# The tables of a routed expert layer built one pass later, and its last pair of passes split

## The reference, cut to what matters

```
logits = rms_norm(x) @ w_router + b_router          # 32 experts
top_v, top_e = top_k(logits, 4);  gates = softmax(top_v)
for each token and each of its 4 experts e:
    g, u = split(xn @ w_gu[e] + b_gu[e])            # 1024 -> 2 x 1024
    a = (min(g, 7) * sigmoid(1.702 * min(g, 7))) * (clip(u, -7, 7) + 1)
    y += gate * (a @ w_down[e] + b_down[e])
out = x + y
```

## Time and profile before

| | |
|---|---|
| median of 3 runs | 1271.04 us (1270.73 to 1271.8) |
| profiled execution | 1271.28 us, span 1269.4 us |
| PE busy | 1224.0 us, 96% of the span |
| DVE, ACT, GpSimd busy | 375.8, 193.6, 16.0 us |
| bytes moved | 463.21 MB, mean 365 GB/s |
| chain that ended last | PE 67%, DMA 30% |

### The profile page before, as it was taken

How to read it: one execution, slowest core, us unless ns; L and a number is a source line. 1 busy time by engine, 2 the same in 40 slices (tenths; PEclk the granted TensorE clock), 3 DMA queues, 4 the chain that set the end, 5 groups by cost and what they waited for, 6 DMA issues and landing times.

```text
span 1269.4 us, 16626 instructions
## 1 busy us (share of the span) xinstructions
PE 1224.0 (96%) x6429; PEld 557.6 (44%) x6429; DVE 375.8 (30%) x918; ACT 193.6 (15%) x438; POOL 16.0 (1%) x28
## 2 busy tenths in 40 slices
PE   9999999999999999989898989999999999998997
PEld 5556778685533443333242333334434333432332
DVE  2555755324441221212121212222212221221222
ACT  3223234302301100110001001101000101000001
POOL 0000000011000000000000000000000000000000
PEclk9999999999999999999999999999999999999999
DMA  9787652498699999999999999999999999999994
GB/s 323 188 249 229 233 168 65 141 345 312 235 413 400 423 428 429 426 429 426 429 427 429 425 429 427 427 421 420 426 426 428 428 430 427 426 429 428 427 426 199
DMA packets 79891, 463.21 MB, mean 365 GB/s; under 512 B 20162, under 2 KB 35290, under 8 KB 54882
## 3 DMA queue, kind: packets, MB, share of 16 engines
q1 hardware_dynamic: 75234, 461.50, 89.8%
q10 hardware_dynamic: 4608, 1.05, 0.5%
HBM read 459.53 MB, written 5.09 MB: 366 GB/s over the span
## 4 chain that ended last, share of the span: by engine, by line
PE 67%; DMA 30%; DVE 1%; ACT 1%; issue 1%; SPq 0%; DVEq 0%; POOL 0%; ACTq 0%; POOLq 0%
DMA arena<-w_gu 22%; PE banks L1243 22%; PE banks L1324 9%; DMA arena<-w_down 8%; PE banks L2196 6%; PE banks L630 5%; PE banks L1214 3%; PE banks L1175 2%; PE banks L810 2%; PE banks L1508 2%; PE banks L574 2%; PE banks L1274 1%; PE banks L1196 1%; PE banks L2215 1%; PE banks L686 1%; PE banks L699 1%
## 5 line engine op out<-in xcount | busy, mean ns | idle before, releaser
L1243 PE MATMUL banks<-arena 128*64 128x512 f32 x1984 | 442.5, 596 | 24.4 <-DMA arena<-w_gu 24.2
L1243 PEld LDWEIGHTS banks<-arena 128*64 128x64 f32 x1984 | 136.8, 137 | 301.2 <-issue 245.9
L1324 PE MATMUL banks<-arena 128*64 128x512 f32 x1024 | 226.4, 592 | 4.7 <-DMA arena<-w_down 4.7
L1421 DVE TENSOR_SCALAR arena<-banks 128x512 f32<-128x512 f32 x32 | 22.1, 692 | 386.9 <-PE banks L1243 366.5
L1324 PEld LDWEIGHTS banks<-arena 128*64 128x64 f32 x1024 | 72.8, 136 | 140.3 <-issue 125.3
L1379 ACT ACTIVATE arena<-arena 128x512 f32<-128x512 f32 x32 | 20.2, 630 | 533.1 <-DVE arena L1421 533.1
L2196 PE MATMUL banks<-arena 128*128 128x512 f32 (+1 forms) x192 | 78.0, 562 | 0.9 <-ACT arena L2266 0.9
L1462 DVE TENSOR_TENSOR arena<-banks,arena 128x528 f32<-128x528 f32 x60 | 42.5, 708 | 75.9 <-PE banks L1214 75.9
L1175 PE MATMUL banks<-arena 128*64 128x512 f32 x256 | 61.3, 599 | 0.9 <-DVE arena L1414 0.9
L630 PE MATMUL banks<-arena 128*128 128x264 f32 x256 | 61.2, 393 | 0.5 <-ACT arena L850 0.5
L1374 DVE TENSOR_TENSOR arena<-banks,arena 128x512 f32<-128x512 f32 x33 | 22.8, 692 | 124.3 <-PE banks L1196 124.3
(11 more groups left out here) (373 smaller groups left out, 934.6 us busy)
## 6 DMA issues: line engine op xcount, KB each, us to landing
arena<-w_gu SPq DMA_DIRECT2D x127, 2048.0 KB, 21.3
arena<-w_down SPq DMA_DIRECT2D x48, 2048.0 KB, 24.1
arena<-w_down SPq DMA_DIRECT2D x16, 1536.0 KB, 24.4
arena<-w_in SPq DMA_DIRECT2D x8, 2048.0 KB, 13.4
arena<-w_down SPq DMA_DIRECT2D x16, 512.0 KB, 25.8
arena<-cache_moba_k SPq DMA_DIRECT2D x16, 256.0 KB, 2.9
arena<-cache_moba_v SPq DMA_DIRECT2D x16, 256.0 KB, 2.8
arena<-w_out SPq DMA_DIRECT2D x2, 2048.0 KB, 12.6
```

The lines of the kernel that those rows point to most:

```text
L1243: mm = nc.tensor.matmul(banks[64 * x:64 * x + 64, BG + b, :], xgT[:, c % 4, 64 * (c // 4):64 * (c // 4) + 64], w[:, D * b + 512 * x:D * b ...
L1324: mm = nc.tensor.matmul(banks[64 * x:64 * x + 64, BY, :], product[:, c, 64 * part:64 * part + 64], w[:, 512 * x:512 * x + 512], start=Fals ...
```

## The change

At the start, the transposes of `triple` move from the gates of pass 0 to those of pass 2, after chunk 1, with the two products of the overflow list behind them (`tables`); the spread of pair 0 moves from behind `gate_up(1)` into the same gates, after chunk 5, and takes its picks from `pick_twin`, which DVE fills, since `pick` by then belongs to later passes. `triple` lies in another place (where `tail_rows` was, so DVE waits for the last read of that), its transposes go to banks 6 and 7. Two products with `ones` become one. DVE's copies and splits of the tables follow `gain_rowsT(2)`.

At the end, pair 15 is split. Its first half (pass 30, rows 0 to 63 of y) is scattered into `acc` by `scatter(..., CAP)` after chunk 1 of `gate_up(32)`, with a wait for its adds; the transposes of `acc` follow after chunks 3, 5 and 7. Its second half (pass 31, rows 64 to 127) goes with pass 32 into one `scatter_tokens`; one spread serves both and stands ahead of `down(31)`. `turn_product(32)` stands between the halves of `down(31)` (`between`), its copy goes to a new buffer `aT_last`, and `down(32)` uses bank BT in place of BY. On ACT `keep_productT(32)` comes ahead of `keep_out(31)`; on DVE the last `select_by_slot` comes ahead of `product(32)`. No load and no store is moved or changed.

```diff
@@ experts_pe: lists, tables
-                    nc.tensor.matmul(banks[:, 7, 3:4], ones, over[:, 2:3], start=True, stop=True)
-                    nc.tensor.matmul(banks[:, 7, 4:5], ones, over[:, 3:4], start=True, stop=True).then_inc(l_found, 1)
-                if c == 5:
+                    nc.tensor.matmul(banks[:, 7, 3:5], ones, over[:, 2:4], start=True, stop=True).then_inc(l_found, 1)
+
+            def tables(c):
+                if c == 1:
                     pe.wait_ge(l_tripled, 1)
                     for x in range(2):
                         for i in range(NT):
                             r = ROWS[i]
-                            mm = nc.tensor.transpose(banks[0:3 * NEXP, 5 + x, P * i:P * i + r], triple[0:r, x, i, :], ident[0:r, 0:r])
+                            mm = nc.tensor.transpose(banks[0:3 * NEXP, 6 + x, 64 * x + P * i:64 * x + P * i + r], triple[0:r, x, i, :], ident[0:r, 0:r])
                     mm.then_inc(l_turned, 1)
+                    pe.wait_ge(l_wanted, 3)
+                    nc.tensor.matmul(banks[0:1, 7, 16:32], const("over_expert")[:, 0:1], over_hot, start=True, stop=True)
+                    nc.tensor.matmul(banks[:, 7, 32:48], const("over_base"), over_hot, start=True, stop=True).then_inc(l_found, 1)
+                if c == 5:
+                    pe.wait_ge(l_read, 2)
+                    pe.wait_ge(S["atkept"], 2)
+                    spread(pe, 0, 2, pick_twin)
...
             gate_up(pe, 1, 1, 1)
-            pe.wait_ge(l_wanted, 3)
-            nc.tensor.matmul(banks[0:1, 7, 16:32], const("over_expert")[:, 0:1], over_hot, start=True, stop=True)
-            nc.tensor.matmul(banks[:, 7, 32:48], const("over_base"), over_hot, start=True, stop=True).then_inc(l_found, 1)
-            pe.wait_ge(l_read, 2)
-            spread(pe, 0, 2)
             gather(pe, 2)
             down(pe, 0, 0, 0, 0)
-            pe.wait_ge(S["stkept"], 2)
             turn_rows(pe, 2)
             turn_product(pe, 1)
-            step(2, 2, (1, 0), 0)
+            gate_up(pe, 2, 2, 0, None, tables)
+            gather(pe, 3)
+            down(pe, 1, 1, 0, 1)
+            pe.wait_ge(S["stkept"], 2)
+            turn_rows(pe, 3)
+            turn_product(pe, 2)
@@ experts_pe: the end
-            def turn_sums(c):
-                i = c // 2
-                if c % 2 == 0 or i >= NT:
+            def sums_before(c):
+                if c == 1:
+                    pe.wait_ge(S["atkept"], LAST)
+                    scatter(pe, PAIRS - 1, LAST - 1, CAP)
+                    pe.wait_ge(S["added"], 4 * PAIRS + 1)
+                if c % 2 == 0 or c == 1:
                     return
+                i = c // 2 - 1
...
-            gate_up(pe, LAST, NEXP - 1, 0, None, turn_sums)
-            down(pe, LAST - 1, 0, NEXP // 2 - 1, 1)
-            turn_product(pe, LAST)
+            def turn_last():
+                pe.wait_ge(S["stkept"], 2 * PAIRS + 2)
+                turn_product(pe, LAST)
+
+            gate_up(pe, LAST, NEXP - 1, 0, None, sums_before)
+            pe.wait_ge(f_added, 4)
+            spread(pe, PAIRS, PASSES)
+            down(pe, LAST - 1, 0, NEXP // 2 - 1, 1, between=turn_last)
+            down(pe, LAST, 1, NEXP // 2 - 1, 0, product=aT_last, bank=BT)
             pe.wait_ge(f_added, 6)
-            scatter_tokens(pe, PAIRS - 1, LAST, last=False)
-            pe.wait_ge(S["atkept"], PASSES)
-            spread(pe, PAIRS, PASSES)
-            down(pe, LAST, 1, NEXP // 2 - 1, 0)
-            scatter_tokens(pe, PAIRS, PASSES, first=False)
+            scatter_tokens(pe, PAIRS, PASSES)
@@ experts_act
+            keep_productT(act, LAST, aT_last)
             keep_out(act, LAST - 1, 1, None)
-            keep_productT(act, LAST)
-            keep_out(act, LAST, 0, None, 1)
+            keep_out(act, LAST, 0, PAIRS, bank=BT)
@@ experts_dve: the start
+            dve.wait_ge(r_tail_cast, 3)
             for x, table in enumerate((rank, weight)):
...
             select(ranks(2))
+            clip_product(dve, 1)
+            product(dve, 1)
+            dve.wait_ge(S["half_down"], 1)
+            picked(expert(2), 0)
+            gain_rowsT(dve, 2)
+            for half in range(2):
+                nc.vector.tensor_copy(pick_twin[0:SPLIT, 64 * half:64 * half + 64], expert(half).broadcast_to([SPLIT, 64]))
             dve.wait_ge(l_turned, 1)
+            dve.wait_ge(l_found, 3)
...
             nc.vector.tensor_copy(parts, whole).then_inc(l_read, 1)
-            clip_product(dve, 1)
-            select_by_slot(dve, 0, slot_of[:, 0:1])
-            product(dve, 1)
-            dve.wait_ge(S["half_down"], 1)
-            picked(expert(2), 0)
-            gain_rowsT(dve, 2)
-            dve.wait_ge(l_found, 3)
...
+            select_by_slot(dve, 0, slot_of[:, 0:1])
             step(2, 0)
@@ experts_dve: the end
             step(LAST - 1, 1, PAIRS - 1, PAIRS - 2)
+            add(dve, PAIRS - 1)
...
             clip_product(dve, LAST)
+            select_by_slot(dve, PAIRS, slot_of[:, PAIRS - 1:PAIRS])
             product(dve, LAST)
-            select_by_slot(dve, PAIRS, slot_of[:, PAIRS:PAIRS + 1], 1)
```

More of the change, by code:

```diff
@@ L1132, in build @@
         xgT_twin, aT_twin = at(twin_at, 4, P), at(wr_at, 4, 2 * AGAIN)
+        aT_last = at(twin_at, 4, P)
         sums_to = [at(d_at + D, D), at(m_at + 3 * D + 3 * D // 2, D), at(out_at, D)]
@@ L1201, in scatter_banks, with scatter @@
             return banks[:, first:first + 2, :]
-        def scatter(pe, pair, passes):
+        def scatter(pe, pair, passes, rows=P):
             pe.wait_ge(S["ykept"], 2 * passes)
@@ L1213, in scatter @@
                 for x in range(2):
-                    mm = nc.tensor.matmul(out[:, x, 0:TOK], y[:, 512 * x + P * c:512 * x + P * c + P], selT, start=True, stop=True)
+                    mm = nc.tensor.matmul(out[:, x, 0:TOK], y[0:rows, 512 * x + P * c:512 * x + P * c + P], selT[0:rows, :], start=True, stop=True)
                 mm.then_inc(S["scat"], 1)
@@ L1289, in spread, with scatter_tokens @@
             mm.then_inc(S["spread"], 1)
-        def scatter_tokens(pe, pair, passes, first=True, last=True):
+        def scatter_tokens(pe, pair, passes):
             pe.wait_ge(S["stkept"], 2 * pair + 2)
@@ L1297, in scatter_tokens @@
                 if i < 2:
-                    nc.tensor.matmul(banks[:, bank, :], selT[:, P * i:P * i + P], y[:, 512 * n:512 * n + 512], start=first, stop=last).then_inc(t_scat, 1)
+                    nc.tensor.matmul(banks[:, bank, :], selT[:, P * i:P * i + P], y[:, 512 * n:512 * n + 512], start=True, stop=True).then_inc(t_scat, 1)
                 elif n == 0:
@@ L1301, in scatter_tokens @@
                         mm = nc.tensor.matmul(banks[32 * x:32 * x + DB, bank, :], selT[:, SEQ:TOK], y[:, 512 * x:512 * x + 512],
-                                              start=first, stop=last, tile_position=(0, 32 * x))
+                                              start=True, stop=True, tile_position=(0, 32 * x))
                     mm.then_inc(t_scat, 1)
@@ L1309, in turn_product, with down @@
             mm.then_inc(S["aturned"], 1)
-        def down(pe, q, parity, nth, half, picks=pick, product=aT):
-            unless_first(pe, S["ykept"], 2 * q)
+        def down(pe, q, parity, nth, half, picks=pick, product=aT, bank=BY, between=None):
+            if bank == BY:
+                unless_first(pe, S["ykept"], 2 * q)
             pe.wait_ge(S["atkept"], q + 1)
@@ L1316, in down @@
                     for x in range(2):
-                        nc.tensor.matmul(banks[64 * x:64 * x + 64, BY, :], picks[0:SPLIT, 64 * half:64 * half + CAP], bias_parts[0:SPLIT, 2 * D + 512 * x:2 * D + 512 * x + 512],
+                        nc.tensor.matmul(banks[64 * x:64 * x + 64, bank, :], picks[0:SPLIT, 64 * half:64 * half + CAP], bias_parts[0:SPLIT, 2 * D + 512 * x:2 * D + 512 * x + 512],
                                          start=True, stop=False, tile_position=(0, 64 * x))
@@ L1323, in down @@
                     for x in range(2):
-                        mm = nc.tensor.matmul(banks[64 * x:64 * x + 64, BY, :], product[:, c, 64 * part:64 * part + 64],
+                        mm = nc.tensor.matmul(banks[64 * x:64 * x + 64, bank, :], product[:, c, 64 * part:64 * part + 64],
                                               w[:, 512 * x:512 * x + 512], start=False, stop=(part == 1 and c == 3), tile_position=(0, 64 * x))
                 mm.then_inc(S["ydone" if part else "half_down"], 1)
+                if between is not None and part == 0:
+                    between()
         def turn_product_again(pe, q):
@@ L1398, in keep_out_again, with keep_out @@
                     kept.then_inc(S["ykept"], 1)
-        def keep_out(act, q, half, scattered, items=None):
+        def keep_out(act, q, half, scattered, items=None, bank=BY):
             act.wait_ge(S["ydone"], q + 1)
@@ L1406, in keep_out @@
             for x in range(2):
```

(11 more changed lines are left out.)

6 lines of the change are left out of this document (3 added, 3 removed).

## The result

The changed kernel takes 1265.79 us (median of 9 runs, 1263.65 to 1267.26), the kernel before in the same comparison 1271.77 (9 runs, 1270.6 to 1278.63). The ratio is 0.9947 [0.9931, 0.9963]. On the 1271.04 of the front that is 1264.3: faster, as forecast, but by more, and 1.3 us under the low end of the range (1265.6).

The account below looks back on a forecast made before the run. DMA was taken as the bound from some 400 us to the end of the weights, then PE; 1271.28 - 1.90 (start) - 2.4 (end) = 1266.98, forecast 1267.0 us, range 1265.6 to 1269.1.

Parts of the forecast that it names:

- The load on half_down 1 carries the stream: Start: the load waiting for half of pass 0's down product goes out 1.90 us earlier, and the stream moves by 1.90.
- The first dip: Start, 364 to 372 us: DMA rate drop losing 1.2 us, to be mostly closed; the second, 380 to 388, stays, a little smaller.
- The 64-row scatter: End, added in gate_up(32): taken at full price, 3.76 us, with half of it (1.9 less) as the bound.
- Two waits of 0.80 and 1.09 at the end: End: PE was to wait 0.8 us after the added scatter and 0.9 before turn_last.
- C-B: End, from PE's wait for pass 30's last w_down piece to the last scatter: forecast 2.4 us shorter, bounds 0 and 3.2.
- DMA 0.8 behind as the next bound: End: the last w_down landing would set the end if PE's late work were cheaper; gain 3.2, 1266.2 us, chance 0.17.
- Rivals B and C: B: start gives nothing, 1268.9 us, chance 0.10. C: end gives nothing, 1269.4, halfway 1268.2; 0.10 for losing most.
- D: Start, gate_up(2): the moved tables make PE wait for DVE and loads starve; slower, 1272.3 us with 8 us wait, chance 0.03.
- Rival E: End: PE's two new waits lower its clock, losing 1.7 us, so 1268.7 us; chance 0.03.
- The term of the start: Start: 1.21 us less before gate_up(1) plus 0.69 before gather(2), so 1.90 us gained; bounds 0 and 3.2.
- the last step of the sum: Whole kernel: sum 1266.98 us; profiled execution 0.24 above the runs' median, put down to scatter, so forecast 1267.0.
- pass for pass the same: Middle passes: each takes the same 29.4 us, only 1.9 us earlier.

Follow-up runs that it names:

- the early fillers: Changed kernel plus useless matmuls between gate_up(1) and gather(2): five (4.49 us) made the stream 5.8 us later; two (1.91 us) 2.0, median 1271.85 us.
- the start alone: Kernel before with only the change's start (tables, first spread, place of `triple`): ratio 0.9989 to before, 1.4 +-0.65 us gained with the clock equal.
- the end alone: Kernel before with only the change's end hunks: last w_down wait of pass 30 to last scatter 44.56 us instead of 46.82.
- filler early 4.5: Changed kernel plus five useless matmuls (4.49 us) between gate_up(1) and gather(2): stream 5.8 us later; last w_down wait of pass 30 to last scatter 46.08 us.
- turn after: Changed kernel with turn_product(32) behind the whole of down(31): last w_down wait of pass 30 to last scatter 44.04 us, 0.41 less.
- its repeat: The changed kernel measured again, unaltered, on the chip of three other runs: median 1265.5 us against 1271.13 for the kernel before.

## Why the prediction was right and wrong

**Right, by its own steps.** The load on half_down 1 carries the stream (the early fillers come back whole, the start alone gives S -2.25). The first dip closed, the second stayed, but smaller. No wait for DVE at chunk 5. The 64-row scatter has the full price, 3.82 beside 3.76, so the row count gives nothing back, as the page "TensorE: Matmul & The Clock Gate" of the Trainium skill (LDWEIGHTS) has it for weight loads. Two waits of 0.80 and 1.09 at the end against 0.8 and 0.9, C-B 2.37 against 2.4. DMA 0.8 behind as the next bound. Rivals B and C fall with the start alone and the end alone. D doesn't show: PE waits nowhere at the tables.

**Rival E is real, but rare.** In the changed kernel's two traces the products behind the two new waits take 3.65 and 3.58 us, the prices of 2.4 GHz. In one of the 11 traces with the added wait of 0.80 us (filler early 4.5) the clock is 0.50 behind it and the end costs 1.63 us more; the prediction had priced such a fall at 1.7. The warning of the Trainium skill that idle gaps between bursts bring the lower clock back ("TensorE: Matmul & The Clock Gate", Why this matters for your kernels) is borne out by that trace and by the three long waits ahead of A; the other ten traces with a wait of 0.80 us show no fall.

**The term of the start was mis-sized: 1.90, and it is 2.20.** "The pieces of that chain touch each other" was read from the chain, where each piece has its length. But a piece in the middle of a stream of products also lengthened its neighbour here, by 0.14 and 0.15 us in the rows above. The chain of the kernel before had shown it: 16 products cost 3.65 or 3.58 behind a small piece, 64 in one piece less than four times that:

```profile
362.54 13.74 PE banks L1243 x64
```

**What put the result outside the range is the last step of the sum**, "in the scatter of a run; I forecast 1267.0". It set the profiled execution beside one median of three runs, 0.24 apart, and took the 341 us ahead of A, and the clock in them, as equal for both kernels. The range held the bounds of the costs but no scatter of the comparison. With the start's true size the same sum gives 1266.7, inside the range, so the start's term alone didn't do it. Runs of before lie between 1268.5 and 1282. Of the 103 whose clock is known 26 were above 1275, all with a mean clock of 0.995 or less. None of the 21 of the changed kernel was that low (0.998 to 1.000). That isn't a gain of the change: of the runs of turn after, whose attention part is the same, six of 12 were.

With the clock equal the change is -4.3 +-0.75 us, its repeat -4.4 +-0.65; the forecast was -4.3, with the start's true size -4.6. So what is shown: the mechanism and the sizes from A on, 4.6 us by the traces. The other 1.4 of the measured 6.0 us is scatter of the comparison, and only in part located. In the profiled executions 0.5 lies ahead of A and 0.5 in before's late landing. Of the 9 runs of before beside the changed kernel three were 1275.89 to 1278.63; without them the median falls from 1271.77 to 1271.36, 0.4 us. That the clock was low in those three is inferred, not seen. In what the rest lies stays open. That the forecast and the clock-equal change are both -4.3 is partly luck, since the start was put 0.3 too low; +-0.75 can't tell them apart.

**The middle was taken too simply** as "pass for pass the same", with a stream that PE can't move. Behind the twice pair the stream is weak once more (371 GB/s from 852 to 858 in before, some 0.7 us lost in every trace), and a fall of the clock ahead of it comes through to S. The slices of the earlier trace rows, 32 us each, hide it. One small step was read too long: the scatter with its adds is 4.50 us by the earlier trace rows (1192.05 to 1196.55), not 4.55, which moves nothing.

## What to carry to other kernels

Where DMA looks full from some point to the end, look for the releases that a load still waits for with a dry queue; windows of 6 to 12 us show them, slices of 32 us don't. PE work ahead of such a release counts one for one. Behind it a small piece cost about a third here, and one larger than the backlog most of its length. At an end where PE, DVE and DMA are within 1 us of each other, one is gained at a time: write down the second-latest before moving the latest. And compare traces from an anchor instruction, with the granted clock of the stretch before it beside them, before a difference of 0.3% is put down to a change. Where a length differs between two executions of one program, look at the granted clock at that place first.

## What the hardware showed that I had not expected

An interruption of a stream of f32 products cost 0.14 to 0.15 us beside its own time in two places; it isn't so everywhere, behind the bias product (L1224) 16 of them take 3.44 us, as in an unbroken stream. The filler's f32 product (128x128 by 512 columns) is two records, 0.45 us each in the chain, which doubled its length. And one stretch of the same program moves all behind it by up to 10 us from one execution to the next (A from 339.5 to 349.8), most of it lost to the clock: the long falls start behind a wait of PE of 2.05 to 3.17 us, while the same wait at 0.69 to 1.55 us had none right behind it.
